# Moving the norm of the linear heads, one 4 KB transfer and three GpSimd operations to other places in the attention stage of a hybrid layer

## What is computed

```python
# linear heads, a chunk at a time
o = o_intra + einsum('bhncd,bhndv->bhncv', q_dec, prev)      # prev: state before the chunk
o_gla = _rmsnorm(o_gla, gla_out_norm) * silu(zg)
# softmax heads, by blocks of queries
p = softmax(where(key_chunk <= q_chunk, q @ k.T * scale, -1e30))
o_mla = p @ v
x = x + concatenate([o_gla, o_mla], -1) @ w_out
h = _rmsnorm(x, mlp_norm)
x = x + square(relu(h @ w_up)) @ w_down
```

## Time and profile before

| | |
|---|---|
| median of 3 runs | 1139.9 us (1135.19 to 1140.2) |
| the profiled execution | 1135.19 us, its span 1133.4 us |
| TensorE matmul, busy | 1104.2 us (97%) |
| VectorE, ScalarE, GpSimd, busy | 778.5, 479.1, 566.9 us |
| four periods of attention, 256 to 425 us | TensorE busy 155.8 of 169 us |

### The profile page before, as it was taken

One profiled execution on the slowest core, in us unless ns is written; L12 is line 12 of the kernel. 1 busy time (PEld: TensorE's weight loads), 2 busy tenths in 40 slices (PEclk: granted clock), 3 DMA queues, 4 the chain that ended last, 5 costly groups with the idle time before them and its releaser, 6 DMA issues.

```text
span 1133.4 us, 14295 instructions
## 1 busy us (share of the span) xinstructions
PE 1104.2 (97%) x5190; PEld 888.9 (78%) x5190; DVE 778.5 (69%) x986; ACT 479.1 (42%) x870; POOL 566.9 (50%) x401
## 2 busy tenths in 40 slices
PE   8999999999899989999999999999999999999998
PEld 7978888765666657887888888888878888888887
DVE  5565767676676661278485775587797988888863
ACT  5353554426757552166323322332334434434441
POOL 2332513238777673048554454444545656555562
PEclk9999999999999999999999999999999999999999
DMA  7242523351221125213534233431789783456632
GB/s 252 69 130 75 167 84 113 106 161 40 75 62 52 57 81 198 75 75 112 176 135 141 106 112 133 141 117 38 258 280 370 238 292 116 137 191 216 211 114 84
DMA packets 101717, 158.38 MB, mean 140 GB/s; under 512 B 9360, under 2 KB 43232, under 8 KB 101648
## 3 DMA queue, kind: packets, MB, share of 16 engines
q1 hardware_dynamic: 100032, 152.83, 41.0%
q10 hardware_dynamic: 1296, 4.46, 1.1%
q0 software_dynamic: 320, 0.19, 0.2%
HBM read 115.47 MB, written 41.94 MB: 139 GB/s over the span
## 4 chain that ended last, share of the span: by engine, by line
PE 81%; DVE 9%; POOL 3%; ACT 3%; issue 2%; DMA 1%; SPq 0%; DVEq 0%; ACTq 0%; POOLq 0%
PE ps L2191 78%; PE ps L2287 1%; POOL tx_lo L1093 1%; DVE m_nm L1888 1%; DVE g_ke L1804 1%; DVE t_all L1963 1%; DVE dr_lo L1963 1%; POOL p_first L1044 1%; DMA raw<-in_w_in_dram 1%; PE ps L2206 1%; POOL a_lo L1093 1%; DMA m_ukv<-in_w_ukv_dram 1%; POOL ua_lo L1098 1%; DVE stage L1963 0%; ACT a_hi L1136 0%
## 5 line engine op out<-in xcount | busy, mean ns | idle before, releaser
L2191 PE MATMUL ps<-dr_hi,dl_hi 128*128 128x512 f32 x448 | 174.5, 390 | 1.6 <-DVE dr_lo L1963 1.6
L1098 POOL TENSOR_TENSOR ua_lo<-up_raw,ua_hi 128x1024 fp32r<-128x1024 f32 x46 | 117.5, 2559 | 115.9 <-ACT ua_hi L1136 115.9
L2191 PE MATMUL ps<-dr_hi,dl_lo 128*128 128x512 f32 x448 | 174.3, 389 | 0.0
L2191 PE MATMUL ps<-dr_lo,dl_hi 128*128 128x512 f32 x448 | 174.3, 389 | 0.0
L1122 POOL TENSOR_TENSOR dl_lo<-l_raw,dl_hi 128x512 fp32r<-128x512 f32 x64 | 101.0, 1602 | 70.4 <-ACT dl_hi L1136 69.9
L1122 POOL TENSOR_TENSOR dl_lo<-s_all,dl_hi 128x512 fp32r<-128x512 f32 x48 | 75.6, 1595 | 58.1 <-ACT dl_hi L1136 57.3
L2191 PEld LDWEIGHTS ps<-dr_hi,dl_hi 128*128 128x128 f32 x448 | 84.1, 188 | 20.3 <-issue 2.8
L2191 PE MATMUL ps<-a_hi,ua_hi 128*128 128x512 f32 x256 | 99.9, 390 | 0.1
L2191 PE MATMUL ps<-a_hi,ua_lo 128*128 128x512 f32 x256 | 99.6, 389 | 0.0
L2191 PE MATMUL ps<-a_lo,ua_hi 128*128 128x512 f32 x256 | 99.6, 389 | 0.0
L2191 PEld LDWEIGHTS ps<-dr_lo,dl_hi 128*128 128x128 f32 x448 | 84.1, 188 | 17.4
(11 more groups left out here) (265 smaller groups left out, 2588.7 us busy)
## 6 DMA issues: line engine op xcount, KB each, us to landing
r_raw<-in_w_down_dram SPq DMA_DIRECT2D x144, 256.0 KB, 3.5
hidden<-stage SPq DMA_DIRECT2D x72, 256.0 KB, 2.0
up_raw<-in_w_up_dram SPq DMA_DIRECT2D x16, 1024.0 KB, 5.5
l_raw<-hidden SPq DMA_DIRECT2D x64, 256.0 KB, 3.5
raw<-in_w_in_dram SPq DMA_DIRECT2D x24, 256.0 KB, 3.5
z_gla<-z_stage SPq DMA_DIRECT2D x16, 256.0 KB, 2.0
raw<-in_w_out_dram SPq DMA_DIRECT2D x16, 256.0 KB, 3.3
xs<-in_x_dram SPq DMA_DIRECT2D x8, 512.0 KB, 9.6
```

Of the source, the lines that this page charges most:

```text
L1098: pool.tensor_tensor(ua_lo[n % UP_RING][:, :, :], up_source(g, product), ua_hi[n % UP_RING][:, :, :].bitcast(F32), ALU.subtract).then_inc( ...
L2191: return pe.matmul(dst, lhsT, rhs, start=start, stop=stop, skip_group_check=onto)
```

## The change

It makes five edits. (1) In `GLA_AT` part 0 of the even chunks moves from S0, place 3, to S1, place 0. (2) On ScalarE `out_rstd` of odd chunks leaves its own place at the end of S0 (after `round_queries`, before `round_keys`) and now stands in part 0 as for the even ones, so in S1 between the exponentials of tiles 2d and 2d + 1. (3) The sync engine issues `chunk_in(2p + 1)` ahead of `maxima(2p + 1)`. (4) On GpSimd the two `add` of a step come after `decays` and `mla_mix_lo` of that step instead of ahead of them, from S1 on; only in L1 does a step hold both, so only there does the order change. (5) `mla_low` of the queries in S1 is written further down with them; nothing in S1 stands between, so its order is the same. On VectorE nothing stands between the two places of part 0, and its order stays.

```diff
-        GLA_AT = ((None, -1, None, 0), (None, 1, 2, None), (3, 4, None, 5), (6, 7, 8, 9), (10, 11, None, 12),
+        GLA_AT = ((None, -1, None, None), (0, 1, 2, None), (3, 4, None, 5), (6, 7, 8, 9), (10, 11, None, 12),
...
-                maxima(2 * p + 1)
                 if p >= 1:
                     chunk_in(2 * p + 1)
+                maxima(2 * p + 1)
...
-                if t == S1 and p + 1 < MH // 2:
-                    mla_low("q", 2 * p + 2)
-                if t != S0:
-                    add(2 * d - 2)
-                    add(2 * d - 1)
                 for place in range(4):
                     if gla_at(d, place):
                         c, n = gla_at(d, place)
...
                 if t == L1 and p >= 1:
                     mla_mix_lo(2 * p - 1)
+                if t == S1 and p + 1 < MH // 2:
+                    mla_low("q", 2 * p + 2)
+                if t != S0:
+                    add(2 * d - 2)
+                    add(2 * d - 1)
...
-                if n == 0 and c % 2:
+                if n == 0 and c >= 1:
                     out_rstd(c - 1)
...
-                if t == S0 and p >= 1:
-                    out_rstd(2 * p - 1)
```

More of the change, by code:

```diff
@@ L1439, in _ @@
                         round_queries(2 * p + 2)
-                if t == S0 and p >= 1:
-                    out_rstd(2 * p - 1)
-                if p + 1 < MH // 2:
                     if t == S1 and p == 0:
```

## The result

The changed kernel takes 1152.31 us (median of 4, 1150.84 to 1156.52), the kernel before 1139.18 (1135.19 to 1140.2): ratio 1.0128, 95% interval 1.0092 to 1.0165. It is slower by 13 us, outside the forecast range of 1134.5 to 1147.5. The profiled execution took 1150.94 us with a span of 1149.2, against 1135.19 and 1133.4.

A forecast was written before the change was run, and what follows sets the result against it. It took TensorE, busy 97% of the span, as the bound. Terms of -1.0, +2.2, +2.2 and -2.5 us for periods 0 to 3 gave +0.9 on 1139.9, so 1140.8 us, range 1134.5 to 1147.5.

The forecast's parts named there:

- rival B: Clock also falls in S1 behind the new waits of periods 1 and 2, 1.7 us each: +4.3, 1144.2 us; chance 0.12.
- the sum that charged the clock nothing for the new waits: Periods 0 to 3 together: -1.0 + 2.2 + 2.2 - 2.5 = +0.9 us.
- the later of my two ends: L0, period 1: the row lands with the chunk at 305.85, not ahead of its data at 304.9.
- rival D: Periods 1 to 3: the chunk doesn't hold the row up, 0.9 us less each: -1.8, 1138.1 us; chance 0.10.
- With a gap under 1 the clock should hold: L2, period 3: TensorE's 3.32 us gap shrinks under 1, so the 1.7 us lost to the slow clock returns.
- A: Periods 1 to 3: nothing is absorbed, VectorE's and GpSimd's chains move along: +8.3, 1148.2 us; chance 0.16.
- C: All periods: VectorE freed from contention with GpSimd: -5.0, or -7.7 with the row not held up; 1132.2 to 1134.9; chance 0.12.
- My last paragraph: Four periods: the prediction is wrong if TensorE's idle time changes by more than 4 us; `m_raw` waits near 1 us.

The follow-up runs named there:

- e3: The kernel before with only GpSimd's `add` moved below `decays` and `mla_mix_lo`, and `mla_low` written further down; 1129.56 us, ratio 0.9898.
- e10: The changed kernel with the row of maxima issued ahead of the chunk again and identity transposes filling TensorE's wait for `og`; 1129.69 us, ratio 0.9926.
- e5: The changed kernel with TensorE doing useless identity transposes in both waits, 14 ahead of `og` and 17 ahead of the row; 1137.09 us, ratio 0.9971.
- e8: The kernel before with 27 identity transposes on TensorE in the 3.32 us gap of period 3; 1135.04 us, ratio 0.9953.
- e9: The changed kernel with the sync engine still waiting for `og`, but then issuing the row before the chunk; 1139.45 us, ratio 1.0001.
- e4: The kernel before with only the norm moved from S0 to S1; 1144.03 us, ratio 1.0035.
- e1: The changed kernel with the row of maxima issued ahead of the chunk again, without waiting for `og`; 1134.0 us, ratio 0.9941.

## Why the prediction was wrong

The medians, taken from one kernel to the next (so that they add up by construction), share out the loss: 1139.85 before, -10.3 by edit 4 (e3), +0.1 by the norm's move at full clock (e10), +7.4 by the row behind the chunk at full clock (e5), +15.2 by the clock (after): 1152.3.

**The step that failed** is rival B's, "at 1.7 a time in two periods" with a chance of 0.12, together with the sum that charged the clock nothing for the new waits. Three things in it were wrong. The price: 1.7 came from a row where the clock came back early, a mean of 0.60 over 4.3 us; behind the new waits it stayed at 0.50 for 10 to 14 us, worth 4.6 to 5.6. No row of the kernel before showed such a length, so the size could not be had from there. The place: period 3 was left out, although the same sum had a wait of 2 us for the row there; it lost 4.6. And the likelihood: rows gave a gap of 3.32 that lowered the clock, and gaps of 0.95 and 1.61 that did not (the second in period 0, where the trace shows 1.00 throughout; B left it out). The new waits of 2.2 and 1.7 us stood between these bounds, so the rows left the question open, and 0.12 took it for nearly settled. With 5 us in each of three periods B would have read 0.9 + 15 = 15.9 over before's 1139.9, or 1155.8, against 1152.3 measured.

**Edits 1 and 2: right.** `og` holds TensorE up for 1.82 (forecast 2.2). In period 3 I had 0.4; it is seen as 0.95 at the weight load. ScalarE's order was as forecast.

**Edit 3: right in mechanism and size.** The row was issued 0.87 after `zv`, and the later of my two ends held: `zg`, issued at 301.28, landed after 3.0 us, at 304.3, and TensorE went on at 304.4. Without the chunk the row needs 1.86 and not 1.24 + 0.2, so rival D's gain was 0.4 too large each time. The wait stood in periods 1 to 3 at 2.08, 2.01 and 1.99. What edits 1 to 3 cost beside the clock is e5 less e3: 2.69, 2.70 and 2.28 (forecast 3.9 - 0.77 = 3.1, twice, and 2.1).

**Edit 4: right.** Forecast -1.0 in period 0, -0.95 in periods 1 and 2, and in period 3, without the +2.1 of the row, -2.9 and -1.7: -7.5 in sum. e3's ledger has -1.50, -1.65, -0.67 and -3.85: -7.7. In medians it is -10.3. That e8 gains 4.5 in the median and only 1.75 in period 3 of the profile suggests why: before's executions lose more to the clock, at one gap or another, than its profiled one does. That was not traced.

**The sum at full clock was nearly right.** e5's periods 1 to 3 and period 0 of the changed kernel give -1.54 + 1.04 + 2.03 - 1.57 = 0.0 for a forecast of +0.9. That it came so near is partly luck: the terms of periods 1 and 3 were each about 1 us off (+1.0 and -1.6 for +2.2 and -2.5), in opposite directions. "With a gap under 1 the clock should hold" did hold, and it was said of the gap behind `w_hi` alone.

**Rivals.** A (nothing is absorbed, 1148.2) has the right side for a wrong reason: at full clock (e5) periods 1 to 3 come to +1.5 together, not to its +8.3. C: `g_ke` of L0 in period 1 did fall from 2.60 to 0.42 us, as forecast, but the sum at full clock is 0.0 and not the -5.0 that C asks for. D is e9's question, answered above. My last paragraph named TensorE's idle time as what would prove me wrong; in the windows it grew by less than 1 us (155.8 to 154.9 busy of 169, later periods cut off). ScalarE's wait of 4.14 for `m_raw` in period 1 went to 1.71, where I had about 1. The sign to name was the granted clock.

## What to carry to other kernels

When an edit gives TensorE a new wait of 1 to 3 us, price the wait and then, by itself, the clock behind it: look for every stretch of the trace where the granted clock is low, how long it stayed low with TensorE busy, and what idle time stood ahead of it. Half of such a stretch is the price of one fall. Here the only stretch before the change lasted 3.4 us and those behind the new waits 10 to 14, so the term needs a range and a chance, not the value of one row. A small transfer that a unit's first matmul needs goes ahead of the large ones in its queue. Where a wait can't be removed, filling it with matmuls that nobody reads shows in one run what the clock costs, and may even be kept.

## What was unexpected of the hardware

Waits of 2 us brought the clock to half for 10 to 14 us, in period 1 from 302.4 to 316 with TensorE fully busy from 304.4, and in periods 1 and 3 the fall came 1.5 and 1.4 us after work had resumed. The Trainium skill (TensorE: Matmul & The Clock Gate, section "Part 1: The HAM clock gate") has a throttled default that activity releases, at a moment that varies from run to run. Its two levels, 2.4 and 1.2 GHz, agree with the rows (1.00 and 0.50). But here it also varies whether the clock falls and for how long: of two equal waits of 1.82 us in one execution of e9, one brought it down, at a price of 5.8 us (6.2 less 0.4), and the other did not; in e4 one of them cost a low stretch of only 3.4 us, from 349.2 to 352.6. That would account for e1's two groups of times, though only one of its executions was profiled. What decides between these was not found out.
